# Attention: the multiplications of the probabilities by the reciprocals of their sums move from VectorE to GpSimd

## The reference, cut to what matters

```
def block(q_blk):
    s = jnp.einsum('bqkgd,bskd->bkgqs', q_blk, k, preferred_element_type=jnp.float32)
    p = jax.nn.softmax(s, axis=-1).astype(v.dtype)
    return jnp.einsum('bkgqs,bskd->bqkgd', p, v)
```

## Time and profile before

| | us |
|---|---|
| median of 3 runs | 3294.25 |
| lowest and highest | 3293.05, 3298.25 |
| the profiled execution | 3294.87 |
| span of its trace | 3293.1 |
| TensorE busy in the span | 2829.3 (86%) |
| VectorE busy | 1833.9 (56%) |
| ScalarE busy | 1188.9 (36%) |
| GpSimd busy | 670.3 (20%) |

### The profile page before, as it was taken

The page is one execution under the profiler, slowest core; times in us unless marked ns, Lnnn a source line. Parts: engine busy times, 40 slices in busy tenths (PEclk is TensorE's granted clock), DMA queues, the critical chain, the costliest instruction groups (busy, mean ns, idle before and its releaser), DMA issues.

```text
span 3293.1 us, 25075 instructions
## 1 busy us (share of the span) xinstructions
PE 2829.3 (86%) x8472; PEld 1533.7 (47%) x8472; DVE 1833.9 (56%) x2733; ACT 1188.9 (36%) x3551; POOL 670.3 (20%) x573
## 2 busy tenths in 40 slices
PE   7999998888997877777779999998898777777777
PEld 6877764444443333333338787444454233323332
DVE  4454555555555555555656755555555555555554
ACT  4344433333333333333343542333333333333333
POOL 1000022222232222222210002222223222222221
PEclk9999999999999999999999999999999999999999
DMA  6544599999999999999995349999999999999998
GB/s 228 184 159 145 189 383 418 431 430 430 431 430 431 431 431 431 431 431 431 431 398 189 128 141 377 418 430 431 430 430 431 431 431 431 431 431 432 430 430 377
DMA packets 139038, 1229.46 MB, mean 373 GB/s; under 512 B 12960, under 2 KB 13728, under 8 KB 68128
## 3 DMA queue, kind: packets, MB, share of 16 engines
q0 software_dynamic: 74016, 1073.77, 76.3%
q1 hardware_dynamic: 61680, 147.99, 12.7%
q10 hardware_dynamic: 3216, 6.12, 0.5%
HBM read 1225.74 MB, written 2.10 MB: 373 GB/s over the span
## 4 chain that ended last, share of the span: by engine, by line
PE 46%; DMA 41%; DVE 7%; ACT 4%; issue 2%; ACTq 0%; POOL 0%; SPq 0%; DVEq 0%; POOLq 0%
DMA ring_sb<-in_peer_uv_dram,idx_cur 39%; PE bank L1256 21%; PE bank L978 15%; PE bank L1025 6%; DVE ring_sb L1779 5%; PE bank L1037 1%; ACT diag L803 1%; ACT shared L794 1%; ACT shared L792 1%; PE bank L1201 1%; DVE w_parts L401 1%; ACT w_parts L395 0%; DMA ring_sb<-in_mlstm_w_out_dram 0%; ACT shared L786 0%; ACT shared L789 0%
## 5 line engine op out<-in xcount | busy, mean ns | idle before, releaser
L1256 PE MATMUL bank<-ring_sb,diag 128*128 128x512 f32 x4080 | 1912.5, 617 | 421.5 <-ACT diag L803 420.7
L1779 DVE CUSTOM_DVE_ANT_0 ring_sb<-ring_sb,arena 128x2048 f32<-128x2048 f32 x512 | 1173.3, 2292 | 1114.3 <-DMA ring_sb<-in_peer_uv_dram,idx_cur 1077.1
L1256 PEld LDWEIGHTS bank<-ring_sb,diag 128*128 128x128 f32 x4080 | 766.3, 195 | 1521.2 <-issue 813.3
L581 POOL DMA_INDIRECT ring_sb<-in_peer_uv_dram,idx_cur x494 | 588.7, 1192 | 1823.4 <-PE bank L1256 1819.1
L786 ACT ACTIVATE shared<-shared 128x1 f32<-128x1 f32 x512 | 103.7, 203 | 1583.0 <-DVE shared L1779 1582.9
L978 PE MATMUL bank<-w_parts,actT_hi 128*128 128x512 f32 x1664 | 520.1, 394 | 9.1 <-DVE w_parts L401 7.5
L978 PEld LDWEIGHTS bank<-w_parts,actT_hi 128*128 128x128 f32 x1664 | 309.3, 188 | 76.5 <-issue 11.2
L401 DVE TENSOR_TENSOR w_parts<-ring_sb,w_parts 128x2048 fp32r<-128x2048 f32 x100 | 229.2, 2297 | 205.3 <-ACT w_parts L395 205.1
L395 ACT CAST w_parts<-ring_sb 128x2048 fp32r<-128x2048 f32 x100 | 190.6, 1909 | 277.7 <-DMA ring_sb<-in_mlstm_w_in_dram 139.6
L978 PE MATMUL bank<-w_parts,actT_lo 128*128 128x512 f32 x640 | 249.9, 391 | 0.0
L803 ACT ACTIVATE diag<-const,shared 128x128 f32<-128x128 f32 x510 | 204.9, 402 | 16.6
(11 more groups left out here) (192 smaller groups left out, 1145.7 us busy)
## 6 DMA issues: line engine op xcount, KB each, us to landing
ring_sb<-in_mlstm_w_in_dram SPq DMA_DIRECT2D x48, 1024.0 KB, 5.0
ring_sb<-in_attn_w_in_dram SPq DMA_DIRECT2D x20, 1024.0 KB, 5.0
ring_sb<-in_mlstm_w_out_dram SPq DMA_DIRECT2D x16, 1024.0 KB, 4.9
arena<-in_peer_wq_dram SPq DMA_DIRECT2D x16, 1024.0 KB, 12.4
ring_sb<-in_attn_w_out_dram SPq DMA_DIRECT2D x16, 1024.0 KB, 4.9
wq_more<-in_peer_wq_dram SPq DMA_DIRECT2D x12, 1024.0 KB, 16.0
ring_sb<-in_peer_uv_dram,idx_cur POOLq DMA_INDIRECT x494
ring_sb<-in_peer_wq_dram SPq DMA_DIRECT2D x4, 1024.0 KB, 8.1
```

The costliest lines, as they stand in the source:

```text
L581: nc.gpsimd.indirect_dma_start(out=uv_slot[at], out_offset=None, in_=uv_rows, in_offset=bass.IndirectOffsetOnAxis(ap=rows_at[:, k:k + 1], ...
L1256: last = mm(acc[n][:, :], diag[slot_of(gu, k)][:, :], v_slot[at][:, n * CH:(n + 1) * CH], start=False, stop=end, skip_group_check=True)
L1779: v.tensor_tensor_reduce(u_slot[at], u_slot[at], xn[b], 1.0, 0.0, ALU.mult, ALU.add, dots[:, k:k + 1]).then_inc(dot_done, 1)
```

## The change

VectorE keeps the reciprocals and signals them with a new semaphore. GpSimd waits for it and does the two multiplications a head. They keep the semaphore `an_ready`, on which TensorE's transposes wait. The roots are now taken apart: four before the multiplications, the fifth between those of heads 5 and 6.

```
+        ars_ready = sem("ars_ready")
...
-            for n in range(5):
+            def root(n):
+
                 pool.wait_ge(msq_ready, n + 1)
                 rsqrt_of(q_r[:, 8 * n:8 * n + 8], q_ms[:, :], 8).then_inc(rq_ready, 1)
+
+            def normalised(h):
+
+                pool.wait_ge(ars_ready, h + 1)
+                for b in range(NB):
+                    nc.gpsimd.tensor_scalar(a_P[h % 2][:, b, :], a_P[h % 2][:, b, :],
+                                            a_rs[:, 2 * (h % 2) + b:2 * (h % 2) + b + 1], None,
+                                            ALU.mult).then_inc(an_ready, 1)
+
+            for n in range(4):
+                root(n)
+            for h in range(6):
+                normalised(h)
+            root(4)
+            for h in range(6, A_HEADS):
+                normalised(h)
...
                 c = slice(2 * (h % 2), 2 * (h % 2) + 2)
                 dve.wait_ge(ap_ready, 2 * h + 2)
-                need(did(v.reciprocal(a_rs[:, c], a_sum[:, c])))
-                for b in range(NB):
-                    v.tensor_scalar(a_P[h % 2][:, b, :], a_P[h % 2][:, b, :],
-                                    a_rs[:, 2 * (h % 2) + b:2 * (h % 2) + b + 1], None, ALU.mult).then_inc(an_ready, 1)
+                v.reciprocal(a_rs[:, c], a_sum[:, c]).then_inc(ars_ready, 1)
```

## The result

The changed kernel takes 3300.77 us (median of 13 runs, 3299.15 to 3306.04) against 3294.28 us (13 runs, 3290.96 to 3298.25). The ratio is 1.0024, with a 95% interval from 1.0017 to 1.0031: 5.6 to 10.2 us slower. The prediction said "within 0.2%" and 3297.2 us, 2.3 us more than before. The measured time lies inside its range, but the loss is almost three times the forecast one and can be told from no change.

The account below looks back on a forecast made before the run. TensorE and VectorE, both full in the attention, were taken as the bound, with the third loop passing TensorE after the change. Terms +0.41, +0.59, +0.97 and +0.3 gave +2.3 us on 3294.87: 3297.2 us, range 3292.0 to 3302.

Parts of the forecast that it names:

- the third loop: Attention, through ScalarE's exponents, the multiplications and TensorE: 3.88 us for two heads before, 4.58 after, against TensorE's 4.33.
- the range's high end: Whole kernel: 3301.8 us at t = 1.1, rounded to 3302; the slowest tail beyond it left out.
- t = 0.64 us: Price of one GpSimd multiplication of 128x256 by a column, taken as half of the 1.28 us product of 128x512.
- The two errors: In the price t: the 128x512 row reads two tensors, not one; halving leaves its fixed part too small.
- the prediction's own formula: Whole change in time, with t the price of one GpSimd multiplication: 10t - 4.4 + 0.3 us.
- To T(6): Up to head 6's transposes, which wait behind the fifth root on GpSimd: +0.41 us (2t - 0.87).
- contention: SBUF at head 4: VectorE's two sums meet GpSimd's pair, one engine waits up to 0.64 us; half taken, +0.3.
- T(6) to T(9): Head 9's transposes come 1.61 us after its exponents, where they came 1.02 after: +0.59 us (2t - 0.69).
- T(9) to T(15): Head 9's to head 15's transposes: three loop turns of 4.58 us, 13.74 against 12.77: +0.97 us (6t - 2.87).
- GpSimd's instruction is slow: Rival, heads 4 to 15: GpSimd becomes the bound, deciding from t = 1.07; 3303.6 us at t = 1.28; chance 0.13.
- Cheap GpSimd: Rival, attention: t = 0.20 us, the copy's row, and VectorE's relief shows; -1.2 us in all, 3293.7 us; chance 0.12.
- the lock-out at every head: Rival: VectorE's small two-input instruction and GpSimd's pair exclude each other, 1.9 us more over heads 5 to 7, 3299.1 us; chance 0.05.

Follow-up runs that it names:

- root behind head 7: The changed kernel with the fifth root behind the multiplications of head 7, no longer of head 5: median 3301.57 us, ratio 1.0023.
- reciprocals first: The changed kernel with VectorE's reciprocals of head h ahead of its maxima of head h+1: 3299.81 us in one run.
- sums first: The changed kernel with VectorE's two sums ahead of head 4's reciprocals: 3304.73 us in one run.
- one instruction a head: The changed kernel with one GpSimd product of 128x512 a head, reciprocal columns broadcast, for two multiplications by a column: median 3295.37 us, ratio 1.0004.

## Why the prediction was wrong

**Right:** the place and, from head 9 on, the mechanism. Only the attention answers, its loss goes to the end one for one, the third loop becomes the bound, TensorE's waits change hands, and heads 0 to 3 cost 0.1 us. That the time still lies in the range is owed to the range's high end, which was set at t = 1.1, and not to the sum.

**The step that failed: t = 0.64 us, "half of the 128x512 product, because that row does the same arithmetic on twice the columns".** It measured 0.925. The two errors were said to point opposite ways; they didn't. Halving the product was low even for a product (0.73 for 128x256). But an instruction that takes its factor from a column is another form, and dearer than one that reads two full tensors: 0.93 against 0.73. The Trainium skill (GPSIMD Engine Reference, Engine selection) calls one-input work roughly line-rate. The copy of 128x256, 0.40 us, is near the 0.42 estimated by it; the multiplication by a column is not. At t = 0.91, half the pair, the prediction's own formula gives 10 x 0.91 - 4.4 + 0.3 = +5.0 us: the price is 2.7 of the 5.3 us by which the stage's loss exceeds the forecast. The rest is below.

**Term by term**, in the stage:
1. To T(6): forecast +0.41, and +0.3 for contention; measured +2.86. The premise that failed is that the mean square comes 1.06 earlier because VectorE has no gap. It came 0.81 later, since VectorE now waits for T(4) (through values and cast), and T(4) itself was 1.85 late. Counted from head 0's transposes it ended at 22.41 us, where the forecast had 20.53. Of these 1.88 us the contention at head 4 is 0.85, for which half of one instruction had been taken; the longer price at head 4, which the sum counted only at head 6, is 0.54; and 0.51 is the lower clock, for which the prediction had no term (4.22 us from T(4) to the mean square, against 3.71 where it did not fall). The price at head 6 is another 0.54.
2. T(6) to T(9): forecast +0.59, measured +1.79. With t = 0.91 it is 1.13. The sentence "TensorE runs from there to the last query transposes without a wait" held only for a short pair: T(7) waited 0.63 us, and it follows T(5) by ScalarE and not T(6). On that path the clock costs 1.69.
3. T(9) to T(15): forecast +0.97, measured 15.93 - 12.77 = +3.16. With t = 0.91 it is 2.59. The loop had been summed as if the reciprocals started when the exponents end; they stand behind the maxima of the next head, 0.15 a turn and 0.30 for the two turns that have them (tried by itself). The other 0.27 is 0.09 a turn: 5.21 measured against 5.12 summed, 0.06 of it between the start of transposes that had to wait and the values behind them (0.49 against 0.43).
4. Behind T(15): nothing forecast, -0.21.

Together 2.86 + 1.79 + 3.16 - 0.21 = 7.60 us.

**The rivals.** "GpSimd's instruction is slow" put its point at t = 1.07, and the price stayed below that; the result came all the same, because nearly all the parts beside the price had the same sign. "GpSimd becomes the bound" did not happen: it waits 14.1 us in the 44 us from 1868. Cheap GpSimd and the lock-out at every head did not happen. Of the lock the Trainium skill (SBUF — State Buffer, Who interferes with whom) says that the one that comes first holds the shared ports for its whole instruction. The trace agrees in part: at head 4 GpSimd's second multiplication, which began while the first sum ran, took 1.77 us and not 0.92; but that sum had begun 0.67 into the first multiplication and was not held, since the two sums took 1.28 together, as before the change (1.29).

**What stays open.** When the clock falls. It fell behind waits of 1.97 (both executions of the changed kernel), 2.33 and 2.79 us, and not behind 1.96, 2.00 (root behind head 7), 2.31 (reciprocals first) and 2.47 (sums first, at head 6). The medians don't show it either: the kernel with the late root, whose profiled stage is 1.57 shorter, measures no faster. So how many of the timed executions lose that time isn't known, and of the 6.5 us between the medians between none and some 1.7 may be due to it.

## What to carry to other kernels

Before work is moved to another engine, price the very form of the instruction that will run there: on GpSimd the factor's form alone took a head's multiplications from 1.82 to 1.18 us, and to 1.04 in one instruction. And where two engines are full but a loop through several engines lies only a little below them, here 3.88 against 4.33 us, the moved work counts at full length in the loop, hand-overs and the place in each queue included. An engine "without a gap" may get one by the change itself: ask what each of its instructions will wait for once the others are late.

## What the runs showed of the hardware that was not expected

- **A factor in a column is dearer than a second tensor on GpSimd.** 128x256: 0.93 us by a column, 0.85 by a constant, 0.73 with a full second tensor, 0.61 with a column repeated by a stride of zero, 0.40 a copy.
- **VectorE's multiplication by a column is held by GpSimd even when its record starts first**: 1897.23 to 1898.03, while GpSimd's product ran from 1897.28 to 1897.89. The Trainium skill (SBUF — State Buffer, Who interferes with whom) lists this form among those that can take the shared ports. 0.352 against 0.805 us agrees with the hold, while its rule that the first to issue goes on does not show in these starts, which lie only 0.05 apart.
- **GpSimd holds a small instruction of VectorE (128x2, usually 0.16 us) to the product's end, but by a column only near its start.** Beside the product (one instruction a head):

```profile
1882.42 1.04 POOL L604 TENSOR_TENSOR ring_sb<-ring_sb,a_stat 128x512 f32<-128x512 f32 x1
1882.87 0.60 DVE L1942 SCALAR_TENSOR_TENSOR a_stat<-a_stat,q_r 128x2 f32<-128x2 f32 x1
```

  It ends 0.01 behind GpSimd's end. Beside a multiplication by a column (the changed kernel, the second one of head 6):

```profile
1882.55 0.94 POOL L605 TENSOR_SCALAR ring_sb<-ring_sb,a_stat 128x256 f32<-128x256 f32 x1
1882.70 0.35 DVE L1943 SCALAR_TENSOR_TENSOR a_stat<-a_stat,q_r 128x2 f32<-128x2 f32 x1
```

  It starts 0.15 in and is held, but ends 0.50 in, while the multiplication goes on for another 0.44. In two other kernels it started 0.09 and 0.18 in, took 0.40 and 0.31, and also ended 0.49 in. Where it starts later it isn't held (reciprocals first):

```profile
1897.01 1.83 POOL L605 TENSOR_SCALAR ring_sb<-ring_sb,a_stat 128x256 f32<-128x256 f32 x2 [1.17 <-DVE a_stat L1955]
1897.53 0.16 DVE L1943 SCALAR_TENSOR_TENSOR a_stat<-a_stat,q_r 128x2 f32<-128x2 f32 x1
```

  It starts 0.52 into the first of the two, which lasts 0.92, and takes its usual 0.16, at ten heads of that kernel. Why the forms differ, no run here tells.
- **The clock can fall behind a wait of 2 us in one execution and not in another**: 0.57 over 4 us against 1.00, products of 1.91 against 1.03 us, 1.30 us lost from T(4) to T(5) and 1.69 to the values behind it. It came in both traces of the changed kernel.
